# Odd-numbered expert weight pieces fetched from ScalarE's DMA queue instead of SyncE's

## What is computed

```python
for e in range(32):
    gu  = ht @ w_gu[e] + b_gu[e]                  # (264, 1024) @ (1024, 2048)
    glu = minimum(gu[:, :1024], 7.0)
    lin = clip(gu[:, 1024:], -7.0, 7.0)
    act = glu * sigmoid(1.702 * glu) * (lin + 1.0)
    out = out + dense_gate[:, e:e+1] * (act @ w_dn[e] + b_dn[e])
```

## Time and profile before

| | before |
|---|---|
| median of three runs | 1331.41 us |
| the profiled execution's own time | 1329.92 us |
| its span, first to last instruction | 1327.9 us |
| TensorE busy | 1294.5 us, 97% |
| bytes moved | 470 MB, of them 457 MB on SyncE's queue |
| DMA rate through most of the mixture | 428 to 430 GB/s |

### The profile page before, as it was taken

One profiled execution on the slowest core, in us unless ns is written; L12 is line 12 of the kernel. 1 busy time (PEld: TensorE's weight loads), 2 busy tenths in 40 slices (PEclk: granted clock), 3 DMA queues, 4 the chain that ended last, 5 costly groups with the idle time before them and its releaser, 6 DMA issues.

```text
span 1327.9 us, 17561 instructions
## 1 busy us (share of the span) xinstructions
PE 1294.5 (97%) x6598; PEld 607.0 (46%) x6598; DVE 456.2 (34%) x1313; ACT 221.7 (17%) x454; POOL 30.1 (2%) x74
## 2 busy tenths in 40 slices
PE   9999998999999999999999999999999999999996
PEld 6879754884743333333333333333333333333333
DVE  4666875145222332222233222233222233222224
ACT  3251224212120110100110100011110011010002
POOL 3000020010000000000000000000000000000000
PEclk9999999999999999999999999999999999999998
DMA  9421624797949999999999999999999999999991
GB/s 312 147 96 32 220 86 152 275 343 314 398 171 401 427 426 429 428 427 429 429 428 428 428 429 428 428 428 429 428 428 428 430 428 428 427 430 428 428 428 75
DMA packets 56683, 469.98 MB, mean 354 GB/s; under 512 B 6884, under 2 KB 7109, under 8 KB 32061
## 3 DMA queue, kind: packets, MB, share of 16 engines
q1 hardware_dynamic: 50554, 457.34, 83.1%
q0 software_dynamic: 3280, 11.40, 2.2%
q10 hardware_dynamic: 2819, 0.83, 0.3%
HBM read 463.84 MB, written 6.29 MB: 354 GB/s over the span
## 4 chain that ended last, share of the span: by engine, by line
PE 87%; DMA 6%; DVE 4%; ACT 1%; issue 1%; DVEq 0%; SPq 0%; POOL 0%; POOLq 0%; ACTq 0%
PE bank L1012 53%; PE bank L554 12%; PE bank L1058 5%; DMA ring<-in_w_gu 5%; PE bank L1025 3%; PE bank L824 3%; PE bank L1044 2%; DVE region_p L1646 2%; PE bank L1038 1%; PE bank L710 1%; PE bank L718 1%; DMA ring<-in_cache_mem_v 1%; PE bank L630 1%; PE bank L903 1%; PE bank L924 1%
## 5 line engine op out<-in xcount | busy, mean ns | idle before, releaser
L1012 PE MATMUL bank<-ring,region_p 128*64 128x512 f32 x2304 | 504.5, 595 | 2.0 <-DMA ring<-in_w_gu 1.3
L1012 PEld LDWEIGHTS bank<-ring,region_p 128*64 128x64 f32 x2304 | 162.9, 137 | 327.5 <-issue 323.3
L1965 DVE TENSOR_SCALAR region_p<-bank 128x512 f32<-128x512 f32 x32 | 22.1, 692 | 615.1 <-PE bank L1044 615.1
L1012 PE MATMUL bank<-region_m,region_p 128*64 128x512 f32 x768 | 169.5, 593 | 0.5 <-DMA region_m<-in_w_gu 0.5
L554 PE MATMUL bank<-hT,ring 128*128 128x264 f32 x512 | 118.7, 388 | 0.0
L1942 DVE TENSOR_TENSOR xT<-xT,bank 128x264 f32<-128x264 f32 x264 | 95.5, 424 | 60.3 <-PE bank L1058 60.3
L1012 PEld LDWEIGHTS bank<-region_m,region_p 128*64 128x64 f32 x768 | 54.3, 137 | 108.7 <-issue 107.3
L554 PEld LDWEIGHTS bank<-hT,ring 128*128 128x128 f32 x512 | 95.5, 190 | 15.8 <-issue 0.4
L1012 PE MATMUL bank<-region_p 128*64 128x512 f32 (+1 forms) x396 | 97.1, 607 | 0.2 <-DVE region_p L1927 0.2
L1409 ACT COPY region_p<-bank 128x264 f32<-128x264 f32 x33 | 12.5, 378 | 475.2 <-PE bank L1038 475.2
L1058 PE MATMUL bank<-region_p 64*128 64x264 f32 x528 | 81.0, 415 | 0.5 <-ACT region_p L1409 0.5
(11 more groups left out here) (382 smaller groups left out, 901.1 us busy)
## 6 DMA issues: line engine op xcount, KB each, us to landing
ring<-in_w_gu SPq DMA_DIRECT2D x96, 2048.0 KB, 20.8
ring<-in_w_dn SPq DMA_DIRECT2D x48, 2048.0 KB, 24.9
region_m<-in_w_gu SPq DMA_DIRECT2D x32, 2048.0 KB, 22.3
region_m<-in_w_dn SPq DMA_DIRECT2D x16, 2048.0 KB, 26.3
ring<-in_w_in SPq DMA_DIRECT2D x6, 2048.0 KB, 15.4
ring<-in_cache_mem_k SPq DMA_DIRECT2D x7, 1024.0 KB, 15.6
ring<-in_cache_mem_v SPq DMA_DIRECT2D x6, 1024.0 KB, 9.7
ring<-in_w_mk SPq DMA_DIRECT2D x2, 2048.0 KB, 7.7
```

What stands on the lines that cost most here:

```text
L1012: ins = pe.matmul(bank[n][u * SLOTS:(u + 1) * SLOTS, :], lhs, rhs, start=start, stop=stop)
L1965: dve.tensor_scalar(xg, bank[0][:, :], 7.0, None, ALU.min).then_inc(sem("glu_clipped"), 1)
```

## The change

SyncE keeps the pieces of even number. ScalarE issues the odd ones from number 9 on: after item u's sigmoid it issues the pieces that take the slots of s = 1 and s = 3 (numbers 6u + 9 and 6u + 11 of the quad's count), and after the copy of the item's result rows the one that takes the slot of s = 5 (6u + 13). ScalarE's loop now runs over quads with four items written out, and the last quad is written once more behind the loop, without the fetches that would lie beyond the end. For this it reads a new number, `last_quad_i`, which VectorE computes with one more small instruction; `routed` counts to 3. The first eight pieces are loaded as before.

```diff
-            sp.wait_ge(sem("routed"), 2)
+            sp.wait_ge(sem("routed"), 3)
             nq = sp.value_load(n_quads_i[0:1, 0:1], ...)
-            for n in range(NSLOT, PIECES * UNROLL):
+            for n in range(NSLOT, PIECES * UNROLL, 2):
                 sp.wait_ge(sem("piece_used"), n - NSLOT + 1)
                 sp.dma_start(piece_slot(n), piece_src(n // PIECES, n % PIECES)).then_inc(sem(f"piece{n % NSLOT}"), 16)
             with sp.Fori(1, nq) as q:
                 e0 = (q * UNROLL) % E
-                for n in range(PIECES * UNROLL):
+                for n in range(0, PIECES * UNROLL, 2):
...
-            with act.Fori(0, n_items) as i:
-                scatter_matrix(i)
-                act.wait_ge(sem("glu_clipped"), i + 1)
-                act.activation(sg, xg, ACT.Sigmoid, scale=1.702).then_inc(sem("sigmoid"), 1)
-                gathered_rows(i + 1)
...
+            last_quad = act.value_load(last_quad_i[0:1, 0:1], ...)
+            def fetch(q, e0, e1, u, s):
+                n = PIECES * u + s + NSLOT
+                item = n // PIECES
+                e = e0 + item if item < UNROLL else e1 + (item - UNROLL)
+                act.wait_ge(sem("piece_used"), PIECES * UNROLL * q + (PIECES * u + s + 1))
+                act.dma_start(piece_slot(n), piece_src(e, n % PIECES)).then_inc(sem(f"piece{n % NSLOT}"), 16)
+            def items(q, last):
+                e0 = (q * UNROLL) % E
+                e1 = (q * UNROLL + UNROLL) % E
+                for u in range(UNROLL):
+                    i = q * UNROLL + u
+                    scatter_matrix(i)
+                    act.wait_ge(sem("glu_clipped"), i + 1)
+                    act.activation(sg, xg, ACT.Sigmoid, scale=1.702).then_inc(sem("sigmoid"), 1)
+                    if not last or u < 3:
+                        fetch(q, e0, e1, u, 1)
+                        fetch(q, e0, e1, u, 3)
+                    gathered_rows(i + 1)
+                    act.wait_ge(sem("act_turned"), i + 1)
+                    act.copy(act_t.rearrange("p c m -> p (c m)"), bank[4][:, :]).then_inc(sem("act_t_ready"), 1)
+                    gathered_columns(i + 1)
+                    act.wait_ge(sem("piece_used"), PIECES * i + PIECES)
+                    act.copy(y_rows, bank[5][:, :]).then_inc(sem("y_ready"), 1)
+                    if not last or u < 2:
+                        fetch(q, e0, e1, u, 5)
+            with act.Fori(0, last_quad) as q:
+                items(q, False)
+            items(last_quad, True)
...
             dve.tensor_scalar(n_quads_i[:, :], cmax[:, 4:5], float(E // UNROLL), None, ALU.mult).then_inc(
                 sem("routed"), 1)
+            dve.tensor_scalar(last_quad_i[:, :], cmax[:, 4:5], float(E // UNROLL), -1.0, ALU.mult, ALU.add).then_inc(
+                sem("routed"), 1)
             dve.tensor_scalar(n_items_i[:, :], cmax[:, 4:5], float(E), None, ALU.mult).then_inc(sem("routed"), 1)
```

More of the change, by code:

```diff
@@ L269, in bass_hymba_step @@
         n_quads_i = sb("n_quads_i", [P, 1], I32)
+        last_quad_i = sb("last_quad_i", [P, 1], I32)
         q_scratch = nc.dram_tensor("q_scratch", (TS, D), F32, kind="Internal").ap()
@@ L1004, in _ @@
                 pe.wait_ge(sem(f"drained{n % 8}"), n // 8 + 1)
-            pe.wait_ge(sem("routed"), 2)
+            pe.wait_ge(sem("routed"), 3)
             n_items = pe.value_load(n_items_i[0:1, 0:1], min_val=E, max_val=5 * E)
@@ L1402, in _ @@
                             sem("gate_exp"), 1)
-            act.wait_ge(sem("routed"), 2)
+            act.wait_ge(sem("routed"), 3)
             n_items = act.value_load(n_items_i[0:1, 0:1], min_val=E, max_val=5 * E)
@@ L1421, in _ @@
             gathered_columns(0)
-            with act.Fori(0, n_items) as i:
-                scatter_matrix(i)
-                act.wait_ge(sem("glu_clipped"), i + 1)
-                act.activation(sg, xg, ACT.Sigmoid, scale=1.702).then_inc(sem("sigmoid"), 1)
-                gathered_rows(i + 1)
[L1427 to L1431, removed]
+            last_quad = act.value_load(last_quad_i[0:1, 0:1], min_val=E // UNROLL - 1, max_val=5 * E // UNROLL - 1)
+            def fetch(q, e0, e1, u, s):
[26 more added lines that the diff above has]
+            items(last_quad, True)
             scatter_matrix(n_items)
@@ L1920, in _ @@
                 wait_drained(dve, "h_tok", i)
-            dve.wait_ge(sem("routed"), 2)
+            dve.wait_ge(sem("routed"), 3)
             dve.wait_ge(sem("gate"), 3)
```

## The result

| | before | changed |
|---|---|---|
| median of 12 runs | 1331.8 us (1328.2 to 1332.8) | 1335.5 us (1332.7 to 1340.1) |
| ratio, 95% interval | | 1.0034 (1.002 to 1.0049) |
| span of the profiled run | 1327.9 us | 1338.1 us |
| item 0 starts at | 387.8 us | 392.6 us |
| M: issue of piece 8 to start of item 31's s = 3 | 897.4 us | 904.2 us |

The change makes the kernel slower by a third of a per cent. A second comparison (the changed kernel 12 times, the one before 35) gave 1.0042 (1.0021 to 1.0062). Forecast were 1337.3 us and a ratio of 1.0044.

A forecast was written before the change was run, and what follows sets the result against it. DMA was taken as the bound, 29.4 us per item against TensorE's 28.65. Late start 0.9, order of arrival 4.9 and VectorE 0.1 made 5.9 us, giving a median of 1337.3 us, range 1330.0 to 1344.0.

The forecast's parts named there:

- Order of arrival: End of the weight stream: two queues share the rate, so piece 189 lands one piece ahead of the last, not two; 4.9 us.
- Late start: Start of the stream: pieces 9 and 11 wait for item 0's sigmoid, making the stream 0.9 us later.
- Where the two meet: End of the loop: item 31's s = 3 starts at 1296.1 us and the last piece lands near 1301.0 us.
- Issues on ScalarE: ScalarE's loop: issues of 0.33 to 0.45 us hide in its waits and idle time, costing nothing.
- VectorE's instruction: One more small instruction before the third count of routed, for which everyone waits: 0.1 us.
- Onset of the waits: Expert loop: TensorE's waits for DMA at s = 3 start near item 18 in place of 26.
- The sum: Whole kernel: 0.9 + 4.9 + 0.1 = 5.9 us more, for a median of 1337.3 us, 0.44% slower.
- Uneven sharing: Rival: queues share unevenly or odd pieces fall in arrears, one more piece of 4.9 us, 1342.2 us; chance 0.15.
- A rate that changes: DMA stream: rate stays 428 GB/s; a lower rate with uneven sharing gives up to 1352 us, within that rival's 0.15.
- Stalls in ScalarE's issues: Rival: loop issues take 5 us each, delaying the copies by 7 us an item, over 1540 us; chance 0.01.
- Two queues cost nothing: Rival: the second queue costs nothing or gains a little rate, 1328.8 us at best or 1331 to 1334; chance 0.18.
- No difference in time: Skill page's reading: several issuers save only issue time and no issue was late, so 1331.4 us; within the 0.18 rival.

The follow-up runs named there:

- after_again: The changed kernel run and profiled once more, nothing altered: M = 903.6 us, ratio 1.0042 to the kernel before.
- one_queue_on_time: Changed kernel's new loops, but SyncE fetches every piece in order of use and ScalarE none: M = 896.6 us, ratio 1.0004 to the kernel before.
- two queues on time: Changed kernel with ScalarE's fetches for s = 1 and s = 3 moved ahead of the scatter-matrix copy: M = 899.6 us, ratio 1.0004 to the kernel before.

## Why the prediction was right

**Order of arrival (4.9 us forecast).** Right in mechanism, shown by three runs: the order alone, without the second queue, costs 5.9 us with the late start and 4.9 by one swap; turned further, it costs 8.6 us more. The pairs and the lone 191 came as worked out. The size is a little more: 189's distance from the last landing fell from 9.8 to 4.6 us, and from the end of the data from 7.7 to 1.4.

Over the four profiles of the changed kernel this last distance is 1.4, 1.4, 2.3 and 2.9 us, and M is 904.2, 904.5, 903.6 and 902.8, while the stream itself lasts 905.7 to 905.9 us in all four. One piece (4.9 us) less than the 7.7 of before would leave 2.8 us; so the pair lands 0 to 1.4 us later behind its data than a single piece did. It goes with the thin end of the stream: in 1 us stretches the shares fall over three to four microseconds where M is long, and from 0.89 to 0.39 and 0.04 in the profile with 902.8. That the 16 engines finish unevenly with two queues fits this, but no run tests it.

The working itself has a slip: it puts 189's issue 23 us ahead of its landing, where its own numbers give 29.4 - 5.9 = 23.5; measured are 23.6. Neither the order nor its price hangs on it.

**Late start (0.9 us).** 0.6 us by the end of the data in the first profile, 0.8 in `after_again` (1298.6 - 392.66 = 905.9).

**Where the two meet.** Forecast were 1296.1 us for item 31's s = 3 and 1301.0 for the last landing, on the time of the profile before. In the changed profile piece 8 is issued 3.4 us later than in that one; less these, the two came at 1297.1 and 1301.7.

**Issues on ScalarE (nothing).** Right: 0.34 us each, 1.97 us of cover left. One of the 92, at 409.32 us, took 1.23 us; it ended at 410.55, ahead of the copy at 411.02.

**VectorE's instruction (0.1 us).** Not measured by itself; in `one_queue_on_time`, which has it, it is lost in an interval of 0.9991 to 1.0016.

**Onset of the waits (near item 18).** Item 19, at 29.37 us per item from there.

**The sum.** 5.8 us forecast in the mixture, without VectorE's 0.1; 6.5 us in M; 3.7 and 4.8 us in the medians, with intervals that take in both. The term that was undersized is the order's, by about 1 us. The median forecast, 1337.3, is 1.8 us from the measured 1335.5; the interval of the ratio is 3.9 us wide, so a miss this small is in part luck, and M is what bears the working out.

**The rivals.** Uneven sharing: no, the pairs looked at land within 0.3 us. A rate that changes: no, 428 to 429 GB/s in each kernel. Stalls in ScalarE's issues: none that delayed a copy. "Two queues cost nothing": nearly true of two queues on time, and not of this change, whose fetches stand behind the sigmoid. That was the part of the prediction in which two causes stood mixed, the share of the rate (half a piece, 2.2 us) and the late issue that puts 189 last but one; only the experiments part them. They don't add up: the late issue alone costs 5.9 us in one queue, the sharing alone 2.2, and both together 6.5, as either puts 189 closer to the end. The Trainium skill (DMA: Bandwidth & Descriptors, "Issuing engines are not separate DMA queues") says that DMAs issued by different engines run on the same 16 DMA engines, so that several issuers save issue time only. The rate agrees, 428 to 429 GB/s with one queue and with two. "No difference in time", the rival read from it, does not hold for this change: with the rate as it was, the time moved with the place of one piece in the order.

## What to carry to other kernels

Where transfers are the bound, the time is set by when the piece that is waited for lands, not only by the rate: issue in the order of use, from a stream that is free when a slot comes free, and not behind compute on another engine. With a second queue the outstanding transfers shared the rate here (two pieces landed together, within 0.3 us, every 9.8 us), and the earlier one of a pair landed later. A disorder does not show while there is a lead; it is paid when the lead is gone. A single swap at the very end cost a whole piece (4.9 us), and an order repaired at the very end gave hardly anything back.

## What the runs showed that I had not expected

A wait of 5.4 us on TensorE was followed by over 4 us at the 1.2 GHz level, which cost 2.1 us more, whereas 13 waits of 0.7 us cost no clock. One long wait was dearer here than the same time in short ones; it was seen in one profile of one kernel.

The stretch ahead of the mixture varies by over 5 us from run to run, with no regard to the kernel: item 0 began between 387.4 us and 392.9 us in thirteen profiles. The granted clock of the first 33 us differs with it (1.00 in the profile shown of before, 0.84 in that of the changed kernel, 0.90 in `after_again`). The clock at item 0 varies too, by 1.4 to 1.7 us, but not in step with it: of the profiles with 1.00 at the start two have a slow item 0 and four a fast one. This scatter is as large as the difference of 6.5 us and makes it hard to see in medians.
